# Causal masks of latent attention as a minimum on VectorE, a bf16 bias product, and three changes of order

## The chip, the cores and the metric

One Trainium2 chip, eight cores. Each core computes half of the positions (16 blocks of 128 out of 32) of one of the four sequences; there is no traffic between cores. The metric is the device time of the slowest core in microseconds.

## The reference

A decoder block on x of shape (4, 4096, 1024), float32:

```python
h = modulate(rmsnorm(x, ln_mix_g), sh1, sc1)          # shifts and scales from silu(c) @ ada_w
proj = h @ w_in                                       # q_lat 256, kv_lat 128, k_rope 32, q/k/v of the window branch, two gates of 1024
y_mla = mla_attention(...)                            # 8 heads, causal over all 4096 positions, keys 64 + 32 rotary, values 64
y_swa = swa_attention(...)                            # 16 heads, window of 128, sinks and a relative bias
merged = sigmoid(gl_a + b) * (y_mla @ w_o_mla) + sigmoid(gl_b + b) * (y_swa @ w_o_swa)
x = x + ga1 * (merged @ w_o)
h = modulate(rmsnorm(x, ln_mlp_g), sh2, sc2)
x = x + ga2 * (square(relu(h @ w_ff1)) @ w_ff2)
return rmsnorm(x, ln_final_g)
```

Latent attention masks as `where(k_idx <= q_idx, s, -inf)` ahead of its softmax.

## The kernel before

Everything lies transposed, channels on the partitions and positions on the free axis, in one SBUF arena whose addresses are planned by the phase in which each buffer lives (`Arena`). A helper class `Sched` records each operation with what it reads and writes and makes the semaphore waits, so that nearly all of an engine's instructions carry one line of the helpers: `mm` L468, `act` L473, `tt` L477, `ts` L486 and L492, `stt` L496, `cp` L500; the reciprocal is L1045, and DMAs are L276. Two stretches (the start up to the end of the x groups, and the keys and queries of the window branch) are captured and put in order by a list scheduler with modelled costs (`arrange`); elsewhere each engine runs in the order of the program text. The stages, with their times in the trace:

1. **Start and x groups, 0 to 148 us.** Adaptation weights `ada0[0..3]` (each 1 MB as bf16, from 2 MB in HBM) and blocks of x (`x_load(i)`, the same size, four buffers, own and other halves in turn) come through GpSimd's queue; small tensors, the weights `wkvxf` (1.8 MB, f32) and table copies through SP's. `ada_mm(i)` makes four columns of `modT`: i = 2, 3 give the scale, from which `wx` (scaled bf16 weights) is made, and i = 0, 1 the shift `sh1`. `bvk` is the bias that the shift adds to the latent projections: 64 f32 matmuls of one column on `wkvxf`. `x_group(i)` makes the mean square of a block with ones-matmuls, projects it by `wx`, normalizes, and builds keys, values and queries of head pair 0. An own group takes about 56 matmuls of 512 columns, the other kind about half.
2. **Latent attention, 148 to 458 us.** For each head pair j, each group c of 512 queries and each head e, the keys come in units of two tiles of 128 (own, other). `mla_front(k)` makes the scores of unit k and `act(..., Exp)` the exponentials `Pt` (bf16); `mla_back(k)` multiplies with the values, three units later in TensorE's order. Three score buffers of two PSUM banks each turn, so front k+3 waits for exponential k. A tile (j, c, e) has 4c full units and three on the diagonal: 1024 columns, 768 (two of 384), and 768 with four key tiles. Each of their eight key tiles has a mask, a further matmul `ident_bf` by `masks[mk]` (128 columns) into the scores: 0 above, −30000 below the diagonal, or a whole tile of either. When a tile ends, VectorE takes the reciprocal of the sums and scales (c even, and pair 3), or ScalarE does it by Ln and Exp. Between the units `do_step` builds the keys, values and queries of the next pair in the accumulator bank that is free, one matmul group and one or two VectorE copies each, placed by modelled times (`pe_t`, `dve_t`). GpSimd makes `ho` (`ho_step`) and the halo (`halo_step`), each one a tensor_tensor and a tensor_scalar of 1024 columns.
3. **Keys and queries of the window branch, 458 to 506 us. Window attention, 506 to 650 us.** 32 rounds `r` of four score banks, four exponentials, Ln and Exp. Rounds 0 to 15 also hold a tile of queries for the second half, rounds 16 to 27 a `gate_tile`: eight matmuls of 512 columns into bank 7 and a copy to `graw`.
4. **Merge, 650 to 850 us.** For each m of 8 output blocks and each g: the gates' matmuls (8 for each of two gates, left out where `graw` holds them, `2 * m + x < 3`), 4 and 8 matmuls of the branches, sigmoids, products.
5. **Output product, 850 to 890 us, and channel mixer, 890 to 1345 us.** `h2_apply(g)` normalizes the residual for the mixer: for each of 8 kc a VectorE product into PSUM bank 6 or 7 and a ScalarE scale and shift into `h2`. That of g = 3 lies between the first `ff1_tile`s: one kc after tile 2, 3, ... 10. An `ff1_tile` is 8 matmuls, Relu on ScalarE into `rl`, a square on VectorE; the buffer of `rl` and the bank of `h2_apply` are chosen by one shared counter `rctr`. The tiles of the first weights go by g, so tile 12 is the first that reads `h2` of g = 3.
6. **Final norm and store, to 1358 us**, through the staging buffer `ost`.

Of the kernel before, what the change touches and what calls it, by code (L numbers as in the profile page):

```python
# [17 lines left out]
NEG = -30000.0  # L18
EPOCH = 3000
# [308 lines left out]
class Arena:  # L328
# [38 lines left out]
    def solve(self):  # L367
# [14 lines left out]
        for _ in range(400):  # L382
# [15 lines left out]
def build_program(plan=None):  # L398
# [31 lines left out]
    with ExitStack() as st:  # L430
# [124 lines left out]

        def kc_src(w, c0, c1):
            return w.rearrange("(kc p) n -> p kc n", p=128)[:, :, c0:c1]
# [6 lines left out]
        S.dma("sp", hv, hv_d, "c4", writes=["hv"])  # L564
        S.dma("sp", relT[0:32, :], relT_d, "c5", writes=["relT"])
        S.dma("sp", eoh[0:32, :], eoh_d, "c6", writes=["eoh"])
        for gg in range(2):
            S.dma("sp", esink[64 * gg:64 * gg + 64, :], sinks_d[:, 8 * gg:8 * gg + 8].partition_broadcast(64), "c8",
                  writes=["esink"], group=True)
# [28 lines left out]
        o_mask = A.alloc(3 * 128 * 2, 0, 3.5, "masks")  # L598
# [66 lines left out]
        bvk = cons(F32, 4)  # L665
        blk_of = ((0, 0, 128), (1, 128, 128), (2, 256, 128), (3, 384, 64))
# [9 lines left out]
        act(esink, esink, AF.Exp, ["esink"], ["esink"])  # L676
# [300 lines left out]

        def v_lhs(t, h):
            return Vb[(h // 2) % 2][:, t, 64 * (h % 2):64 * (h % 2) + 128]
# [14 lines left out]
        def mla_front(k):  # L994
# [4 lines left out]
            for (t, off, w, qo, mk) in u:  # L999
                out = PS(sb + off // 512)[:, off % 512:off % 512 + w]  # L1000
                kd = [("Kpe0", 0, t // 4), ("Kdup0", t // 4)] if b == 0 else [("Kpe1", e, t // 4)]
                mm(out, Kb[b][e][:, 128 * t:128 * t + 128], qt[:, 512 * c + qo:512 * c + 512], True, mk is None,
                   [("K%d" % b, e, t // 4), qk + (c, 0), qk + (c, 1)] + kd,
                   [("ps", sb + off // 512)])
                if mk is not None:
# [11 lines left out]
            act(dst, src, AF.Exp, [("ps", sb), ("ps", sb + 1)], [("P", pi)], scale=SC_MLA)  # L1017

# [143 lines left out]
        o_gr = A.alloc(12 * 512 * 4, 4.6, 5, "graw")  # L1162
        graw = V(o_gr, F32, 12 * 512, [12, 512])
# [121 lines left out]
        for r in range(34):  # L1285
            if r < 32:
# [7 lines left out]
                elif r < 28:  # L1294
# [20 lines left out]
        for m in range(8):  # L1315
# [5 lines left out]
            for g in range(4):  # L1321
# [19 lines left out]
                for x, (gt, gk) in enumerate(((gA, "gA"), (gB, "gB"))):  # L1341
                    if 2 * m + x < 3:
# [35 lines left out]

        def h2_apply(g, kcs=range(8)):
            cs = slice(512 * g, 512 * g + 512)  # L1380
            for kc in kcs:
                rb = rctr[0] % 2
                rctr[0] += 1
                tt("dve", PS(6 + rb)[:, :], x1[:, kc, cs], rst[g % 2], ALU.mult, [("x1", g, kc), ("rst", g % 2)],
                   [("ps", 6 + rb)])
                act(h2[:, kc, cs], PS(6 + rb)[:, :], AF.Identity, [("ps", 6 + rb), "mod2"], [("h2", g)],
                    scale=gm2[:, kc:kc + 1], bias=sh2[:, kc:kc + 1])
# [33 lines left out]
        o_ost = A.alloc(2 * 8 * 512 * 4, 9, 9, "ost")  # L1421
# [29 lines left out]
        for hf in range(4):  # L1451
            pa, pbb = PI_FF[hf]
            for i4 in range(2):
# [167 lines left out]
```

How the kernel before makes its waits and increments, by code:

```python
                def body(eng):  # L312
                    for (waits, fn, sig) in self.prog[e]:
                        for (k, v) in waits:
                            eng.wait_ge(self.sems[k], v)
                        if fn is None:
                            continue
                        ins = fn(eng)
                        if sig is not None:
                            ins.then_inc(self.sems[sig[0]], sig[1])
```

## Time and profile before

| what | us |
| --- | --- |
| median of three runs | 1360.99 (1359.23 to 1580.57) |
| the profiled execution, its own time | 1360.09 |
| its span, first to last instruction, slowest core | 1358.5 |
| spans of the eight cores | 1353.1 to 1358.5 |
| TensorE busy | 1252.3 (92%) |
| ScalarE busy | 649.8 (48%) |
| VectorE busy | 627.5 (46%) |
| GpSimd busy | 200.4 (15%) |

TensorE's busy time counts a matmul from its first column to a modelled end and so looks fuller than it is; the distance from one matmul to the next is the better measure. All rows are those of core 5, the slowest. PEclk is the granted TensorE clock as a share of 2.4 GHz.

### The profile page before, as it was taken

How to read it: one execution, taken by the hardware profiler on the slowest of the kernel's cores; microseconds unless marked ns; L12 is line 12 of the kernel's file. 1: busy time of each engine (PE TensorE's matmuls, PEld its weight loads, DVE VectorE, ACT ScalarE, POOL GpSimd, SP SyncE). 2: the span in 40 equal slices, each digit the busy share in tenths (PEclk: the TensorE clock that was granted, in tenths of full speed). 3: DMA queues.
4: the chain of work that ended last, by engine and by line, in shares of the span. 5: the costliest groups of instructions: out<-in, count | busy, mean ns of one | idle time of the engine just before them, and what ended most of it. 6: DMA issues, size and time to landing. Idle time of an engine off the chain costs nothing.

```text
span 1358.5 us, 20199 instructions; the slowest of 8 cores (1353.1 to 1358.5 us)
## 1 busy us (share of the span) xinstructions
PE 1252.3 (92%) x6826; PEld 588.7 (43%) x6826; DVE 627.5 (46%) x849; ACT 649.8 (48%) x924; POOL 200.4 (15%) x174
## 2 busy tenths in 40 slices
PE   0599798999999999998899999979999999999997
PEld 0344344445454553332344444434444444444445
DVE  0549665655565333444322223653443443443457
ACT  0258788889889417777322223853003103202343
POOL 3000355310045001000342320010000000000000
PEclk9889899999999999999899999999999999999999
DMA  9993756130283206020462333383223205000015
GB/s 170 213 122 55 136 135 125 48 63 1 32 119 83 33 0 55 1 28 34 97 76 28 32 59 93 94 118 69 31 26 68 31 1 92 3 1 1 1 62 187
DMA packets 97507, 89.12 MB, mean 66 GB/s; under 512 B 37200, under 2 KB 83072, under 8 KB 97280
## 3 DMA queue, kind: packets, MB, share of 16 engines
q0 software_dynamic: 72640, 51.03, 28.3%
q1 hardware_dynamic: 24768, 36.81, 8.5%
q8 instruction: 58, 0.95, 0.3%
q14 instruction: 41, 0.34, 0.1%
HBM read 127.02 MB, written 8.41 MB: 100 GB/s over the span
## 4 chain that ended last, share of the span: by engine, by line
PE 85%; DVE 5%; ACT 4%; issue 4%; DMA 2%; SPq 1%; DVEq 0%; ACTq 0%; POOL 0%; POOLq 0%
PE psb L468 85%; ACT arena L473 3%; DVE arena L477 2%; DVE arena L496 1%; DMA arena<-sinks 1%; DVE arena L1045 1%; SPq L276 1%; DVE psb L477 0%; DMA scr<-arena 0%; DVE arena L500 0%; ACT L473 0%; DVE arena L486 0%; DVEq L315 0%; ACTq L315 0%; POOL arena L477 0%
## 5 line engine op out<-in xcount | busy, mean ns | idle before, releaser
L468 PE MATMUL psb<-arena 128*128 128x512 bf16 (+7 forms) x6826 | 1252.3, 347 | 98.4 <-ACT arena L473 52.8
L468 PEld LDWEIGHTS psb<-arena 128*128 128x128 bf16 (+3 forms) x6826 | 588.7, 101 | 761.8 <-issue 216.0
L473 ACT ACTIVATE arena<-psb 128x1024 bf16<-128x1024 f32 (+5 forms) x595 | 434.2, 787 | 413.9 <-PE psb L468 411.0
L477 DVE TENSOR_TENSOR arena<-psb,arena 128x512 f32<-128x512 f32 (+2 forms) x222 | 145.1, 660 | 276.3 <-ACT arena L473 181.4
L477 DVE TENSOR_TENSOR arena<-arena 128x512 bf16<-128x512 f32 (+3 forms) x150 | 111.1, 742 | 159.8 <-ACT arena L473 159.3
L496 DVE SCALAR_TENSOR_TENSOR arena<-psb,arena 128x512 f32<-128x512 f32 (+1 forms) x168 | 121.8, 725 | 136.0 <-PE psb L468 135.8
L473 ACT ACTIVATE arena<-arena 128x512 f32<-128x512 f32 (+4 forms) x211 | 139.3, 675 | 89.0 <-DVE arena L496 63.8
L473 ACT ACTIVATE arena<-psb,arena 128x512 f32<-128x512 f32 (+2 forms) x113 | 79.9, 709 | 156.9 <-PE psb L468 143.2
L500 DVE CAST arena<-psb 64x512 bf16<-64x512 f32 (+1 forms) x134 | 92.1, 688 | 86.2 <-PE psb L468 84.9
L477 POOL TENSOR_TENSOR arena<-arena 128x512 bf16<-128x512 f32 (+1 forms) x56 | 96.9, 1730 | 229.3 <-DVE arena L477 113.0
L1045 DVE RECIPROCAL arena<-psb 64x512 f32<-64x512 f32 x20 | 67.1, 3355 | 26.5 <-PE psb L468 25.9
L276 POOL DMA_DIRECT2D arena<-w_ff x16 | 13.0, 822 | 309.0 <-PE psb L468 248.3
L496 DVE SCALAR_TENSOR_TENSOR arena<-arena 128x512 f32<-128x512 f32 (+6 forms) x75 | 53.8, 728 | 8.1 <-ACT arena L473 3.8
L276 POOL DMA_DIRECT2D arena<-win x19 | 17.2, 909 | 150.7 <-PE psb L468 150.7
L276 POOL DMA_DIRECT2D arena<-ada_w x12 | 11.0, 918 | 165.8 <-PE psb L468 165.0
L492 POOL TENSOR_SCALAR arena<-arena 128x1024 bf16<-128x1024 f32 x24 | 29.1, 1214 | 5.8 <-POOL arena L477 3.9
L473 ACT ACT_TABLE_LOAD x5 | 6.4, 1283 | 42.3 <-DMA arena<-sinks 29.8
L477 DVE TENSOR_TENSOR psb<-arena 128x512 f32<-128x512 f32 x32 | 21.9, 692 | 0.3 <-ACT arena L473 0.3
L500 DVE COPY arena<-psb 128x512 f32<-128x512 f32 (+3 forms) x22 | 12.9, 586 | 19.7 <-PE psb L468 19.7
L486 DVE TENSOR_SCALAR arena<-arena 128x448 bf16<-128x448 f32 (+4 forms) x19 | 9.6, 533 | 3.9 <-ACT arena L473 3.1
L276 POOL DMA_DIRECT2D arena<-xo x4 | 3.6, 892 | 52.1 <-PE psb L468 52.1
L500 DVE CAST arena<-arena 128x1024 f32<-128x1024 int32 (+1 forms) x3 | 3.5, 1157 | 11.6 <-DMA arena<-pos 11.4
(14 smaller groups left out, 32.9 us busy)
## 6 DMA issues: line engine op xcount, KB each, us to landing
arena<-w_ff POOLq DMA_DIRECT2D x16, 1024.0 KB, 10.9
arena<-ada_w POOLq DMA_DIRECT2D x12, 1024.0 KB, 15.1
arena<-xo SPq DMA_DIRECT2D x16, 512.0 KB, 4.8
arena<-xo SPq DMA_DIRECT2D x4, 2048.0 KB, 8.1
out<-arena SPq DMA_DIRECT2D x12, 512.0 KB, 3.0
arena<-xo POOLq DMA_DIRECT2D x4, 1024.0 KB, 29.5
arena<-xs POOLq DMA_DIRECT2D x4, 1024.0 KB, 31.9
arena<-xs SPq DMA_DIRECT2D x8, 512.0 KB, 4.4
```

Of the source, the lines that this page charges most:

```text
L276: return eng.dma_start(out=out, in_=in_, **kw)
L468: S.op("pe", lambda e: e.matmul(out, lhsT=lhsT, rhs=rhs, start=start, stop=stop), reads=R, writes=Wr, sig=sig, cost=cost_of("pe", out, lhsT))
L473: S.op("act", lambda e: e.activation(out=out, in_=in_, func=func, **kw), reads=R, writes=Wr, cost=cost_of("act", out))
L477: S.op(eng, lambda e: e.tensor_tensor(out=out, in0=in0, in1=in1, op=op), reads=R, writes=Wr, cost=cost_of(eng, out, in0, in1))
L486: is not None else e.tensor_scalar(out=out, in0=in0, scalar1=s1, scalar2=None, op0=op0),
L492: S.op(eng, lambda e: e.tensor_scalar(out=out, in0=in0, scalar1=s1, scalar2=s2, op0=op0, op1=op1), reads=R, writes=Wr, cost=cost_of(eng, o ...
L496: S.op("dve", lambda e: e.scalar_tensor_tensor(out=out, in0=in0, scalar=scalar, in1=in1, op0=op0, op1=op1), reads=R, writes=Wr, cost=cost_ ...
L500: S.op(eng, lambda e: e.tensor_copy(out=out, in_=in_), reads=R, writes=Wr, cost=cost_of(eng, out, in_))
L1045: S.op("dve", lambda e_, ab=ab, hy=hy, hs=hs: e_.reciprocal(out=R[hy, :], in_=PS(ab)[hs, :]), reads=[("ps", ab)], writes=[("rr", e)])
```

## The change

- In latent attention, groups c = 1, 2, 3 lose their mask matmuls. In their place `cap` takes the elementwise minimum of the exponentials and a table `caps`, which holds 0 where a key is hidden and the largest bf16-sized number elsewhere. It is a VectorE tensor_tensor of 128 x 256 bf16, in place on `Pt`, right behind the exponential: one on each of the first two diagonal units and two on the third. Group c = 0 keeps its masks. `caps` is made once by four small tensor_scalars.
- In the start, the small SP loads (with `sinks`) go ahead of `wkvxf`; `x_load(1)` goes ahead of `ada0` 0 and 1; `bvk` is made from a bf16 copy of the weights (two ScalarE copies) and a shift split into two bf16 parts, 32 bf16 matmuls of two columns, summed by two VectorE reductions; the exponential of the sinks waits for `bvk`.
- Window rounds 28 to 31 take gate tiles too, so the merge leaves four gates out of m = 0 and 1.
- `h2_apply(3)`: the VectorE product runs two kc ahead of the ScalarE part, with its own bank choice, no longer through `rctr`.
- `ost` takes the place of `h2`; the arena's search may take more trials.

```diff
-        S.dma("sp", wkvxf, kc_src(win_d, 0, QC + KVC), "wkvx", writes=["wkvxf"])
         S.dma("sp", hv, hv_d, "c4", writes=["hv"])
...
+        S.dma("sp", wkvxf, kc_src(win_d, 0, QC + KVC), "wkvx", writes=["wkvxf"])
...
-        x_load(0)
+        for i in range(2):
+            x_load(i)
         for i in (0, 1):
             ada0_load(i)
-        for i in range(1, NXB):
+        for i in range(2, NXB):
             x_load(i)
...
+        for q in range(2):
+            act(wkvb[:, 4 * q:4 * q + 4, :], wkvxf[:, 4 * q:4 * q + 4, :], AF.Copy, ["wkvxf"], [("wkvb", q)])
+        cp("dve", sh1s[:, :, 0], sh1, [("mod", 0), ("mod", 1)], [("sh1s", 0)])
+        tt("dve", sh1s[:, :, 1], sh1, sh1s[:, :, 0], ALU.subtract, [("mod", 0), ("mod", 1), ("sh1s", 0)], [("sh1s", 1)])
         for (col, c0, M) in blk_of:
             for kc in range(8):
-                mm(PS(6)[0:M, col:col + 1], wkvxf[:, kc, c0:c0 + M], sh1[:, kc:kc + 1], kc == 0, kc == 7,
-                   ["wkvxf", ("mod", 0), ("mod", 1)], [("ps", 6)])
-            cp("dve", bvk[0:M, col:col + 1], PS(6)[0:M, col:col + 1], [("ps", 6)], ["bvk"])
+                mm(PS(6)[0:M, 2 * col:2 * col + 2], wkvb[:, kc, c0:c0 + M], sh1s[:, kc, :], kc == 0, kc == 7,
+                   [("wkvb", kc // 4), ("sh1s", 0), ("sh1s", 1)], [("ps", 6)], sig=(kc == 7 and col == 3))
...
-        act(esink, esink, AF.Exp, ["esink"], ["esink"])
+        act(esink, esink, AF.Exp, ["esink", "bvk"], ["esink"])
...
+        for sl, mk in ((0, 0), (1, 1), (2, 0), (3, 2)):
+            ts("dve", caps[:, sl // 2, sl % 2, :], masks[:, mk, :], 0.0, BIG, ALU.is_ge, ALU.mult, ["masks"], ["caps"])
+
+        def cap(pi, off, step, sel):
+            v = Pt[pi][:, off:off + 2 * step].rearrange("p (a b) -> p a b", a=2)[:, :, 0:128]
+            tt("dve", v, v, caps[:, sel, :, :], ALU.min, [("P", pi), "caps"], [("P", pi)])
...
-                if mk is not None:
+                if mk is not None and c == 0:
                     mm(PS(sb + off // 512)[:, off % 512:off % 512 + 128], ident_bf, masks[:, mk, :], False, True,
                        ["ident", "masks"], [("ps", sb + off // 512)])
...
             act(dst, src, AF.Exp, [("ps", sb), ("ps", sb + 1)], [("P", pi)], scale=SC_MLA)
+            if c > 0 and len(u) == 2 and u[0][4] is not None:
+                cap(pi, 0, 512, u[1][4] - 1)
+            elif c > 0 and len(u) == 4:
+                cap(pi, 0, 256, 0)
+                cap(pi, 512, 128, 1)
...
-                elif r < 28:
+                elif r < 32:
                     q = r - 16
                     gate_tile(q // 8, q % 4, q // 4 % 2)
...
-                        if 2 * m + x >= 3:
+                        if 2 * m + x >= 4:
...
                     if hf == 0 and i4 == 0 and 3 <= n_ < 11:
-                        h2_apply(3, (n_ - 3,))
+                        if n_ == 3:
+                            h2_norm(3, 0)
+                            h2_norm(3, 1)
+                        h2_shift(3, n_ - 3)
+                        if n_ - 1 < 8:
+                            h2_norm(3, n_ - 1)
```

## Rows read from the trace of the kernel before

**Rows 1.** The page: busy us of each engine, its share of the span, instructions
```profile
PE 1252.3 (92%) x6826; PEld 588.7 (43%) x6826; DVE 627.5 (46%) x849; ACT 649.8 (48%) x924; POOL 200.4 (15%) x174
```
**Rows 2.** Busy time by stage: stretch, its length, then each engine's us (instructions)
```profile
core 5: us, PE busy (x) PEld busy (x) DVE busy (x) ACT busy (x) POOL busy (x), PEclk, DMA share, GB/s
0.00:71.80 71.80, 24.05 (x210) 16.91 (x210) 19.28 (x31) 11.49 (x11) 12.51 (x21) 0.92 1.08 190
148.00:458.00 310.00, 289.23 (x1970) 150.41 (x1968) 177.11 (x186) 273.23 (x307) 99.41 (x65) 0.99 0.44 83
890.00:930.00 40.00, 32.94 (x143) 14.12 (x142) 16.47 (x25) 17.28 (x29) 3.66 (x5) 0.91 0.91 137
```
**Rows 3.** Waits from 148 to 458 us: engine line waited for, us, times, longest
```profile
ACT arena L473 <- PE psb L468: 33.4, 68, 1.7
```
**Rows 4.** Groups by form from 148 to 458 us: count, busy us, mean ns
```profile
L473 ACT ACTIVATE arena<-psb 128x1024 bf16<-128x1024 f32 x224 | 214.4, 1037 | 27.3 <-PE psb L468 25.8
L477 POOL TENSOR_TENSOR arena<-arena 128x1024 f32<-128x1024 f32 x24 | 56.4, 2351 | 41.2 <-DMA arena<-xo 22.7 <-DMA arena<-xs 18.3
L492 POOL TENSOR_SCALAR arena<-arena 128x1024 bf16<-128x1024 f32 x24 | 29.1, 1214 | 5.8 <-POOL arena L477 3.9 <-PE psb L468 1.9
```
**Rows 5.** TensorE in order of time from 1200 us: start, us, matmuls
```profile
1199.71 85.63 PE L468 MATMUL psb<-arena 128*128 128x512 bf16 x396
```
**Rows 6.** VectorE groups by form over the span: count, busy us, mean ns
```profile
L477 DVE TENSOR_TENSOR arena<-arena 128x2048 bf16<-128x2048 bf16 x8 | 9.7, 1218 | 0.1
L477 DVE TENSOR_TENSOR arena<-psb,arena 128x4 f32<-128x4 f32 x12 | 1.9, 160 | 42.0 <-PE psb L468 42.0
```
**Rows 7.** A tile of c = 1, pair 2, in order of time, 319.6 to 323.9 us
```profile
318.33 3.35 DVE L1045 RECIPROCAL arena<-psb 64x512 f32<-64x512 f32 x1
319.73 4.66 ACT L473 ACTIVATE arena<-psb 128x1024 bf16<-128x1024 f32 x5 [1.22 <-PE psb L468]
321.78 0.69 DVE L477 TENSOR_TENSOR arena<-psb,arena 64x512 bf16<-64x512 f32 x1
```
**Rows 8.** The two-SBUF-input VectorE product in 311 to 314 and in 233 to 237 us
```profile
L477 DVE TENSOR_TENSOR arena<-arena 64x512 bf16<-64x512 f32 x1 | 0.7, 684 | 3.3 <-ACT arena L473 3.3
L477 DVE TENSOR_TENSOR arena<-arena 64x512 bf16<-64x512 f32 x1 | 2.5, 2509 | 3.2 <-ACT arena L473 3.2
```
**Rows 9.** The start in order of time, 0 to 165 us
```profile
29.77 1.28 ACT L473 ACT_TABLE_LOAD   x1 [29.77 <-DMA arena<-sinks]
61.80 3.54 PE L468 MATMUL psb<-arena 128*128 128x1 f32 x16 [2.31 <-DVE arena L477]
82.09 1.62 PEld L468 LDWEIGHTS psb<-arena 128*128 128x128 bf16 x9 [0.41 <-issue]
89.28 1.90 ACT L473 ACTIVATE arena<-arena 128x2048 bf16<-128x2048 bf16 x1
```
**Rows 10.** The load of x block 2 (issued at 6.90 us): KB, us to landing
```profile
arena<-xo POOLq DMA_DIRECT2D x1, 1024.0 KB, 62.8
```
**Rows 11.** ScalarE in order of time: window rounds 24, 28 and 31 begin
```profile
612.27 2.06 ACT L473 ACTIVATE arena<-psb 128x512 bf16<-128x512 f32 x4 [1.21 <-PE psb L468]
...
629.74 2.07 ACT L473 ACTIVATE arena<-psb 128x512 bf16<-128x512 f32 x4 [1.21 <-PE psb L468]
...
639.43 2.05 ACT L473 ACTIVATE arena<-psb 128x512 bf16<-128x512 f32 x4
```
**Rows 12.** The mixer's first tiles: waits from 890 to 930 us, then order of time
```profile
PE psb L468 <- ACT arena L473: 7.0, 2, 6.1
909.80 0.69 DVE L477 TENSOR_TENSOR psb<-arena 128x512 f32<-128x512 f32 x1
912.62 0.69 DVE L477 TENSOR_TENSOR psb<-arena 128x512 f32<-128x512 f32 x1
917.20 9.00 PE L468 MATMUL psb<-arena 128*128 128x512 bf16 x32 [6.09 <-ACT arena L473]
```
**Rows 13.** TensorE group of one-column bf16 matmuls over the span: count, busy us, mean ns
```profile
L468 PE MATMUL psb<-arena 128*128 128x1 bf16 x384 | 11.4, 163 | 37.8 <-ACT arena L473 36.1 <-DVE arena L477 1.3
```

More of the change, by code:

```diff
@@ L18 @@
 NEG = -30000.0
+BIG = float(2.0 ** 128 - 2.0 ** 120)
 EPOCH = 3000
@@ L381, in solve @@
         order = list(best[2])
-        for _ in range(400):
+        for _ in range(3000):
             if best[0] <= self.limit:
@@ L554, in build_program @@
         S.dma("sp", gains, gains_d, "c2", writes=["gains"])
+        S.dma("sp", hv, hv_d, "c4", writes=["hv"])
+        S.dma("sp", relT[0:32, :], relT_d, "c5", writes=["relT"])
+        S.dma("sp", eoh[0:32, :], eoh_d, "c6", writes=["eoh"])
+        for gg in range(2):
+            S.dma("sp", esink[64 * gg:64 * gg + 64, :], sinks_d[:, 8 * gg:8 * gg + 8].partition_broadcast(64), "c8",
+                  writes=["esink"], group=True)
         def kc_src(w, c0, c1):
@@ L563, in build_program @@
         S.dma("sp", wkvxf, kc_src(win_d, 0, QC + KVC), "wkvx", writes=["wkvxf"])
[L564 to L569, printed above, removed]
         o_ada0 = A.alloc(4 * 8192, 0, 0, "ada0")
@@ L590, in x_load @@
                   ("xst", i % NXB), writes=[("xst", i % NXB)])
-        x_load(0)
+        for i in range(2):
+            x_load(i)
         for i in (0, 1):
             ada0_load(i)
-        for i in range(1, NXB):
+        for i in range(2, NXB):
             x_load(i)
         S.dma("pool", ident_bf, ident_d, "c9", writes=["ident"])
-        o_mask = A.alloc(3 * 128 * 2, 0, 3.5, "masks")
+        o_mask = A.alloc(7 * 128 * 2, 0, 3.5, "masks caps")
+        caps = V(o_mask + 3 * 128 * 2, BF16, 4 * 128, [2, 2, 128])
         masks = V(o_mask, BF16, 3 * 128, [3, 128])
@@ L668, in build_program @@
             for kc in range(8):
-                mm(PS(6)[0:M, col:col + 1], wkvxf[:, kc, c0:c0 + M], sh1[:, kc:kc + 1], kc == 0, kc == 7,
-                   ["wkvxf", ("mod", 0), ("mod", 1)], [("ps", 6)])
-            cp("dve", bvk[0:M, col:col + 1], PS(6)[0:M, col:col + 1], [("ps", 6)], ["bvk"])
+                mm(PS(6)[0:M, 2 * col:2 * col + 2], wkvb[:, kc, c0:c0 + M], sh1s[:, kc, :], kc == 0, kc == 7,
+                   [("wkvb", kc // 4), ("sh1s", 0), ("sh1s", 1)], [("ps", 6)], sig=(kc == 7 and col == 3))
+        for (c0, c1, M) in ((0, 3, 128), (3, 4, 64)):
+            S.op("dve", lambda e, c0=c0, c1=c1, M=M: e.reduce_sum(
+                out=bvk[0:M, c0:c1], in_=PS(6)[0:M, 2 * c0:2 * c1].rearrange("p (a b) -> p a b", b=2),
+                axis=mybir.AxisListType.X), reads=[("ps", 6)], writes=["bvk"], cost=0.2)
         mm(PS(6)[0:16, 0:128], relT[0:32, :], eoh[0:32, :], True, True, ["relT", "eoh", "bvk"], [("ps", 6)])
@@ L1161, in build_program @@
         qsT = [V(o, BF16, 4 * T, [4, T]) for o in o_qs]
[L1162 to L1163 removed]
+        o_gr = A.alloc(16 * 512 * 4, 4.6, 5, "graw")
+        graw = V(o_gr, F32, 16 * 512, [16, 512])
         ksT = V(o_ks, BF16, T)
@@ L1377, in tail_ones, with h2_norm, h2_shift @@
             act(rst[q % 2][:, 0:w], rst[q % 2][:, 0:w], AF.Exp, [("rst", q % 2)], [("rst", q % 2)], scale=-0.5)
+        def h2_norm(g, kc):
+            cs = slice(512 * g, 512 * g + 512)
+            tt("dve", PS(6 + kc % 2)[:, :], x1[:, kc, cs], rst[g % 2], ALU.mult, [("x1", g, kc), ("rst", g % 2)],
+               [("ps", 6 + kc % 2)])
+        def h2_shift(g, kc):
+            act(h2[:, kc, 512 * g:512 * g + 512], PS(6 + kc % 2)[:, :], AF.Identity, [("ps", 6 + kc % 2), "mod2"],
+                [("h2", g)], scale=gm2[:, kc:kc + 1], bias=sh2[:, kc:kc + 1])
         def h2_apply(g, kcs=range(8)):
-            cs = slice(512 * g, 512 * g + 512)
             for kc in kcs:
[L1382 to L1387, printed above, removed]
+                h2_norm(g, kc)
+                h2_shift(g, kc)
         xre_load(1)
@@ L1420, in build_program @@
         it2 = 0
-        o_ost = A.alloc(2 * 8 * 512 * 4, 9, 9, "ost")
+        o_ost = o_h2
+        if S.live:
+            S.region(o_ost, 2 * 8 * 512 * 4, ["ost"])
         def final_apply(q, kcs=range(8)):
```

7 lines of the change are left out of this document (5 added, 2 removed).

## The prediction

> **What bounds the kernel now.** I read the page first, then busy time by stage, then the waits and the order of time inside the stages that the change touches. The page has TensorE busy for 92% of the span and no other engine above 48% [rows 1]. So work saved on TensorE counts wherever TensorE is the engine that the others wait for, and the question for each edit is whether it is so in its stage.
>
> By stage [rows 2]: up to 71.8 us TensorE is busy for only 24 us while the DMA share is 1.08, so the start waits for data. Latent attention, 148 to 458 us, has TensorE busy for 289 of 310 us and ScalarE for 273 us, so two engines are near their limit there. From 890 to 930 us TensorE has 7 us of idle time and a mean granted clock of 0.91 of 2.4 GHz. The waits of latent attention say which of the two engines leads: ScalarE waited 33.4 us for TensorE's scores, in 68 waits [rows 3]. TensorE leads, by some 10% of the stage, and gains less once ScalarE's exponentials (1024 columns in 1.04 us, 224 of them, 214 us busy [rows 4]) become the pace.
>
> **Masks (groups 1 to 3).** 8 mask matmuls in each tile, 3 groups, 8 heads: 192 matmuls of 128 columns. 396 matmuls of 512 columns take 85.63 us [rows 5], 0.216 us each, so 128 columns take 0.054 us, and 192 take 10.4 us. All of it is on TensorE's queue. ScalarE has on average 33.4 / 24 = 1.4 us of waiting per tile of these groups to give up, more than the 0.43 us saved, so I count the 10.4 us in full before the costs below.
>
> The minimum: the trace has no such instruction. The nearest are a bf16 product of 2048 columns, 1.218 us, and a sum of 4 columns, 0.160 us [rows 6]. The line through both gives 0.29 us for 256 columns. The bounds are 0.16 us and, for full f32 speed, the 0.68 us of a 512-column product with both inputs in SBUF [rows 8]. I take 0.29, as the type and kind are those of the first row. 96 of them are 28 us on VectorE, which is busy 177 of 310 us [rows 2], so there is room on average. What counts is the delay of `mla_back(k)`, which now waits for exponential and minimum. Between front k and back k TensorE issues three fronts and three backs, 12 matmuls of 0.216 us or 2.6 us, and the exponential uses 1.04 us of it. That leaves 1.5 us for 0.29 us (0.6 us for the two of the last unit). Even where ScalarE leads, front k+3 (0.43 us) still stands between. With an idle VectorE the minimum costs nothing.
>
> VectorE is not always idle. Two cases can cost:
> - *Behind a reciprocal.* In the tile (c = 1, e = 0) the reciprocal of the group-0 tile lies ahead: it starts at 318.33 and takes 3.35 us, its scaling ends at 321.78 + 0.69 = 322.47 [rows 7]. The first diagonal exponential is the first of the five from 319.73, so it ends about 320.75, and its back matmul comes about 1.4 us later, at 322.1. With the minimum it can start at 322.8: 0.7 us late. Four pairs give 2.8 us; the tile (c = 1, e = 1) of pair 3, which also follows a reciprocal, 0.6 us more. Longer tiles have eight or more full units first, time enough for 4.1 us. Sum 3.4 us.
> - *Behind GpSimd.* The same VectorE product takes 0.684 us in one place and 2.509 us where GpSimd is inside a tensor_tensor [rows 8]. GpSimd's two instructions are 2.35 and 1.21 us long, 24 of each in this stage [rows 4], 86 of 310 us, and lie mostly in 160 to 246 us and in pair 3. There, 52 minima meet a busy GpSimd with a chance of about a half; a hold of up to 2.35 us exceeds the slack of 1.2 us that is left in a minority, by some tenths. I take 3 us, between 0 (all hidden) and 31 us (third rival).
>
> Behind a waiting minimum stand the copies of `do_step`. The next tile's first back, which needs their bank, comes four iterations later, over 3 us, so they cost nothing while that holds. `caps` is four small instructions in an idle stretch: nothing. Latent attention: −10.4 + 3.4 + 3.0 = **−4.0 us**.
>
> The Trainium skill (GPSIMD Engine Reference, section on specifications) says that GpSimd shares its SBUF interfaces with VectorE and contends with VectorE instructions that have two SBUF inputs; the minimum is one. The trace agrees with its 2.509 us.
>
> **The start.** ScalarE's first instruction waits 29.77 us for `sinks`, because these lie behind `wkvxf`, and with it wait `scT`, all `ada_mm` and the table chain of VectorE [rows 9]. Then x group 0 runs; the bias takes 4 x 3.54 us of f32 matmuls from 61.80 to about 75.8; only then x group 1; and the ones-matmuls of group 2 start at 82.09 [rows 9]. In the new order x groups 0 and 1 are through, and the bias is 32 bf16 matmuls of 11.4 / 384 = 0.03 us [rows 13], 1 us in all. The two copies of weights are at most 1.9 us each [rows 9] on an idle ScalarE. What sets the time next is the landing of x block 2: 6.90 + 62.8 = 69.7 us [rows 10]. The same bytes lie ahead of it as before and the DMA share is full up to there, so it doesn't move. With the square of half a block, 1.9 us [rows 9], its ones-matmuls start at 71.8, 10.3 us earlier. TensorE will have idled for some microseconds before, and then steps at half speed at first, as at 917.20, where 32 matmuls took 9.00 us [rows 12] and 32 x 0.216 = 6.9 would do: 2.1 us lost. **−8.2 us.** Bounds: 0 (the planner leaves the order as it was or data come later) and −14 us (the f32 bias alone, everything else in its shadow).
>
> **Gates in rounds 28 to 31.** Rounds with a gate take (629.74 − 612.27) / 4 = 4.37 us, without one (639.43 − 629.74) / 3 = 3.23 us, there ScalarE leads [rows 11]. Four rounds grow by 1.14 us, 4.5 us. The merge loses four groups of 8 x 0.216 us, 6.9 us. **−2.4 us**; at worst 0, at best −6.9.
>
> **The mixer's first tiles.** One kc of `h2_apply` costs 912.62 − 909.80 = 2.82 us, a closed loop of VectorE, ScalarE, Relu and square, against 8 x 0.216 = 1.73 us of an `ff1_tile`. TensorE so waits 7.0 us for ScalarE, and the slow restart at 917.20 loses 2.1 us [rows 12]. With the product two kc ahead, each engine has two instructions per tile, about 1.3 to 1.4 us, below 1.73. So TensorE no longer waits: **−9.1 us**. At worst half is left, −4.5. The stages behind are full of TensorE, nothing later eats it.
>
> `ost` on `h2`, whose last readers are long done, costs nothing; nor does the arena's search.
>
> **Sum.** 4.0 + 8.2 + 2.4 + 9.1 = 23.7 us from 1360.1 us of the profiled execution (span 1358.5): **1336 us**. The median shown, 1361, is 0.9 us above that execution, no more. The change is 1.8%. A measurement of this kernel tells about 2% from no change, that is below 1334 us or above 1388 us.
>
> **Rivals.**
> 1. *VectorE hides all minima.* For it: 1.5 us of slack. Against it: the reciprocal ahead [rows 7]. Then latent attention gives 10.4, in sum 30.1: 1330 us.
> 2. *The start gives nothing*, since the data or the halved clock set it or the list scheduler places the groups otherwise. For it: the DMA share of 1.08 [rows 2]. Against it: group 1 stood 14 us behind the bias. 1336.4 + 8.2: 1345 us.
> 3. *Slower: GpSimd holds the minima.* GpSimd is inside an instruction for 86 / 310 = 28% of the stage; 96 minima, with a mean rest of about 1.1 us, are 30 us of holds if none is hidden. Latent attention then costs −10.4 + 3.4 + 30 = +23, in sum 1360.1 − 19.7 + 23 = 1363 us. It decides where the slack behind the exponential is below the hold; TensorE's lead over ScalarE makes the slack, and the change takes that lead away. Against it: in three fifths of the stage GpSimd is idle.
> 4. *`h2_apply` keeps half of its stall*, as the squares of the tiles come in between on VectorE: 1341 us.
>
> The rule of the Trainium skill on the shared interfaces (GPSIMD Engine Reference, specifications) is the mechanism of the third rival, and would make it 1363 us if it bit each time.
>
> **Chances.** Forecast 0.55 (its own range 1329 to 1344), rival 1 0.18, rival 2 0.13, rival 3 0.05, rival 4 0.09. Leaving out rival 3 and the tails, the range is **1326 to 1349 us**. Faster by over 2%: rival 1 at 0.15 of its 0.18, and 0.19 of the forecast: 0.34. Slower by over 2%: 0.01. Within: 0.65.
>
> **What would show it.** Right: no mask matmuls beyond c = 0 (64 in all, of 256); latent attention about 306 us long; ScalarE's wait for TensorE well under 33 us; minima of 0.29 us, a few of 2 us; x group 2 at about 72 us; rounds 28 to 31 of 4.4 us; no TensorE wait near 905 us. Wrong: minima behind which TensorE waits in most tiles; latent attention as long as before; x group 2 later than 76 us.

## The result, and the profile after

The changed kernel takes 1371.32 us in the median of 5 runs (1368.48 to 1515.14), the kernel before 1359.97 us (1357.88 to 1580.57) beside it. The ratio is 1.008, with a 95% interval of 1.0061 to 1.0099: 0.8% **slower**, little but clearly apart from no change, and not the 1336 us of the forecast. Some executions of any kernel here are disturbed on some cores and take up to 16% longer; every ratio is taken from undisturbed ones, and where they spoil a median, the lowest time stands in its place.

The profiled execution took 1369.8 us, with a span of 1368.1 us on core 4. The cores lie between 1361.0 and 1368.1 us, so it isn't one late core. The page, busy us of each engine, its share and instructions, to be held against [rows 1]:

```profile
PE 1238.9 (91%) x6602; PEld 567.0 (41%) x6602; DVE 664.9 (49%) x953; ACT 651.2 (48%) x925; POOL 201.2 (15%) x174
```

TensorE has 224 instructions and 13.4 us of work less, and the kernel got longer: the difference is waiting. Which stage it is in shows when each core's span is cut at ScalarE's first and last exponential of latent attention (medians over the eight cores, read from ScalarE's order of time):

| us | up to it | latent attention | behind it |
|---|---|---|---|
| before | 148.9 | 305.3 | 901.4 |
| after | 141.2 | 333.1 | 890.0 |
| forecast of the change | −8.2 | −4.0 | −11.5 |
| measured change | −7.7 | **+27.8** | −11.4 |

Two of three stages come out nearly as forecast. Latent attention, where the mask matmuls were taken away, is 32 us off. Its busy time by stage in the changed kernel (columns as in [rows 2], second window chosen to hold the whole stage of core 4):

```profile
148.00:458.00 310.00, 261.80 (x1615) 126.72 (x1614) 205.83 (x268) 249.75 (x281) 93.90 (x60) 0.98 0.36 73
143.00:478.00 335.00, 286.41 (x1766) 139.34 (x1766) 213.58 (x284) 272.43 (x307) 99.37 (x64) 0.98 0.37 73
```

TensorE was idle 310.00 − 289.23 = 20.8 us in the stage before [rows 2] and is idle 335.00 − 286.41 = 48.6 us now: 27.8 us more. What it waits for, from the waits of the stage (us, times, longest), first in the kernel before, 148 to 458 us:

```profile
PE psb L468 <- DVE arena L477: 11.0, 8, 1.9
PE psb L468 <- ACT arena L473: 8.1, 10, 1.1
```

and in the changed kernel, 145 to 478 us:

```profile
ACT arena L474 <- PE psb L469: 58.5, 65, 4.5
DVE arena L478 <- ACT arena L474: 49.1, 35, 5.1
PE psb L469 <- DVE arena L501: 22.0, 20, 3.3
PE psb L469 <- DVE arena L478: 16.7, 14, 1.9
PE psb L469 <- ACT arena L474: 7.3, 9, 1.1
```

Line 501 is a copy of the projections that `do_step` builds between the attention tiles; line 478 is the helper of the products and of the minima. TensorE didn't wait for such a copy before and now does so 20 times, 22.0 us in all. That is TensorE's largest new row, and it doesn't name the minimum. (ScalarE's 58.5 us, against 33.4 in [rows 3], reads as the echo: its scores come late because TensorE does, as in the rows below.)

One such place in the order of time of the changed kernel (start, us, engine and line, count, then the wait before it):

```profile
338.94 0.29 DVE L478 TENSOR_TENSOR arena<-arena 128x256 bf16<-128x256 bf16 x1 [2.90 <-ACT arena L474]
339.64 0.29 DVE L478 TENSOR_TENSOR arena<-arena 128x256 bf16<-128x256 bf16 x1 [0.41 <-ACT arena L474]
339.86 0.68 DVE L501 CAST arena<-psb 128x512 bf16<-128x512 f32 x1
340.69 1.67 PE L469 MATMUL psb<-arena 128*128 128x512 bf16 x7 [1.69 <-DVE arena L501]
341.86 1.02 ACT L474 ACTIVATE arena<-psb 128x1024 bf16<-128x1024 f32 x1 [1.61 <-PE psb L469]
```

VectorE stands 2.90 us at a minimum whose exponential isn't there yet, then 0.41 us at the next. Only behind them does it reach the copy of a build, at 339.86. TensorE, which needs the bank that this copy empties, has stood 1.69 us when it goes on, and ScalarE 1.61 us for its scores. GpSimd has no part in it. Here it has one:

```profile
430.00 1.41 DVE L501 CAST arena<-psb 64x512 bf16<-64x512 f32 x2 [0.63 <-PE psb L469]
432.07 2.91 DVE L478 TENSOR_TENSOR arena<-arena 128x256 bf16<-128x256 bf16 x2 [0.67 <-ACT arena L474]
432.46 2.37 POOL L478 TENSOR_TENSOR arena<-arena 128x1024 f32<-128x1024 f32 x1
435.01 0.69 DVE L501 CAST arena<-psb 128x512 bf16<-128x512 f32 x1
435.85 4.35 PE L469 MATMUL psb<-arena 128*128 128x512 bf16 x16 [3.16 <-DVE arena L501]
437.44 1.02 ACT L474 ACTIVATE arena<-psb 128x1024 bf16<-128x1024 f32 x1 [4.22 <-PE psb L469]
```

Two minima that need 0.29 us each take 2.91 us; they end at 434.98, just behind GpSimd's tensor_tensor (432.46 + 2.37 = 434.83). The copy starts at 435.01, and TensorE has waited 3.16 us for it.

The three copies of this place read PSUM and take their usual 0.7 us, the first two beside another tensor_tensor of GpSimd (428.78 to 431.13 us). A third cost shows in the clock that TensorE was granted behind its wait (columns as in [rows 2]):

```profile
435.30:438.60 3.30, 2.75 (x7) 1.09 (x8) 2.62 (x5) 1.02 (x1) 2.65 (x2) 0.50 0.39 116
```

This is the lower of the two levels, 1.2 GHz. It came at 435.25 us, while TensorE stood idle.

### The profile page after: what moved, and what is told of

It is laid out like the page before. It is cut to its first block, busy times and chain, and to the rows that moved or that the text cites. A ratio compares the mean times of both kernels' runs of the same rounds, so it can differ in the third digit from the quotient of the medians.

```text
span 1368.1 us, 19972 instructions; the slowest of 8 cores (1361.0 to 1368.1 us)
## 1 busy us (share of the span) xinstructions
PE 1238.9 (91%) x6602; PEld 567.0 (41%) x6602; DVE 664.9 (49%) x953; ACT 651.2 (48%) x925; POOL 201.2 (15%) x174
## 4 chain that ended last, share of the span: by engine, by line
PE 80%; DVE 6%; ACT 5%; issue 5%; DMA 3%; another core or an unknown queue 1%; POOL 0%; ACTq 0%; DVEq 0%; POOLq 0%; SPq 0%
PE psb L469 80%; ACT arena L474 5%; DMA arena<-xo 2%; DVE arena L478 2%; DVE arena L501 2%; DVE arena L1071 1%; DVE arena L497 1%; DMA scr<-arena 0%; POOL arena L277 0%; ACTq L316 0%; DVEq L316 0%; ACT L474 0%; POOL arena L478 0%; POOLq L316 0%
## 5 line engine op out<-in xcount | busy, mean ns | idle before, releaser
L469 PE MATMUL psb<-arena 128*128 128x512 bf16 (+6 forms) x6602 | 1238.9, 351 | 121.4 <-DMA arena<-ada_w 28.7
L469 PEld LDWEIGHTS psb<-arena 128*128 128x128 bf16 (+1 forms) x6602 | 567.0, 99 | 793.1 <-issue 250.3
L478 DVE TENSOR_TENSOR arena<-arena 128x512 bf16<-128x512 f32 (+4 forms) x247 | 149.5, 611 | 195.2 <-ACT arena L474 180.3
L474 ACT ACTIVATE arena<-arena 128x512 f32<-128x512 f32 (+6 forms) x217 | 145.0, 684 | 127.7 <-DVE arena L497 53.3
L474 ACT ACTIVATE arena<-psb,arena 128x512 f32<-128x512 f32 (+2 forms) x109 | 76.9, 709 | 133.3 <-PE psb L469 130.6
L497 DVE SCALAR_TENSOR_TENSOR arena<-arena 128x512 f32<-128x512 f32 (+6 forms) x75 | 53.9, 727 | 12.8 <-ACT arena L474 8.4
L501 DVE COPY arena<-psb 128x512 f32<-128x512 f32 (+1 forms) x22 | 15.0, 681 | 6.3 <-PE psb L469 6.3
L504 POOL MEMSET arena<- 128x2048 bf16 (+4 forms) x6 | 4.3, 779 | 24.7 <-PE psb L469 20.2
L501 DVE CAST arena<-arena 128x1024 f32<-128x1024 int32 (+2 forms) x4 | 2.2, 562 | 11.4 <-DMA arena<-pos 11.2
```

Of the source, the lines that this page charges most:

```text
L469: S.op("pe", lambda e: e.matmul(out, lhsT=lhsT, rhs=rhs, start=start, stop=stop), reads=R, writes=Wr, sig=sig, cost=cost_of("pe", out, lhsT))
L474: S.op("act", lambda e: e.activation(out=out, in_=in_, func=func, **kw), reads=R, writes=Wr, cost=cost_of("act", out))
L478: S.op(eng, lambda e: e.tensor_tensor(out=out, in0=in0, in1=in1, op=op), reads=R, writes=Wr, cost=cost_of(eng, out, in0, in1))
L497: S.op("dve", lambda e: e.scalar_tensor_tensor(out=out, in0=in0, scalar=scalar, in1=in1, op0=op0, op1=op1), reads=R, writes=Wr, cost=cost_ ...
L501: S.op(eng, lambda e: e.tensor_copy(out=out, in_=in_), reads=R, writes=Wr, cost=cost_of(eng, out, in_))
L504: S.op(eng, lambda e: e.memset(ap, val), writes=Wr)
```

## The experiments

Times are medians. The interval of a ratio is about ±0.002 (from ±0.001 to ±0.005), or 3 us, and a difference between two kernels is good to 3 or 4 us. The kernel before gave 1359.9 to 1360.5 us beside all of them.

**One part at a time.** The theory: the minimum costs, the other edits give what was forecast. First the changed kernel with its mask matmuls back in all groups and no minima:

```diff
-                if mk is not None and c == 0:
+                if mk is not None:
...
-            if c > 0 and len(u) == 2 and u[0][4] is not None:
-                cap(pi, 0, 512, u[1][4] - 1)
-            elif c > 0 and len(u) == 4:
-                cap(pi, 0, 256, 0)
-                cap(pi, 512, 128, 1)
```

> The changed kernel with the mask matmuls of groups 1 to 3 put back and the minima left out; all other parts of the change stay. The two traces put latent attention 26 us longer after the change, the start 5 to 8 us shorter and everything behind latent attention 12 us shorter. If these are separate, this kernel takes 1360 - 7 - 12 = 1341 us. If the longer latent attention came with the new start (other data in flight, a shifted clock) and not from the minima, it stays near 1366 us.

Its lowest time is 1338.07 us (of 1338.07 to 1561.92), and it has no interval. The same kernel once more:

> The kernel of the first experiment again (all of the change but the minima), for its interval on the chip of this group: 1339 us, ratio to the kernel before 0.985.

Measured: 1340.21 us (1339.87 to 1341.37), ratio 0.9848 (0.9834 to 0.9863). This beats both kernels, and puts the price of minima against masks at 1371.3 − 1340.2 = **31.1 us**. TensorE's waits in it, 145 to 478 us (which holds some 30 us behind its latent attention), are those of before, with no wait for a copy among them:

```profile
PE psb L469 <- DVE arena L478: 9.4, 6, 1.8
PE psb L469 <- ACT arena L474: 8.1, 10, 1.1
```

The opposite, the kernel before with only the minimum in place of the masks of groups 1 to 3:

> The kernel before with the minimum in place of the mask matmuls of groups 1 to 3 and nothing else of the change. If the minima cost what the traces say, 1360 + 26 = 1386 us. If the loss needs the other parts, 1356 us as forecast for this edit alone.

Measured: ratio 1.0275 (1.0235 to 1.0315), by which it takes about 1397 us; the lowest time is 1393.5 us. Latent attention has a median of 335.5 us over the cores, and the same new row:

```profile
PE psb L469 <- DVE arena L501: 23.0, 21, 3.1
PE psb L469 <- DVE arena L478: 22.8, 16, 3.1
```

And neither masks nor minima in groups 1 to 3. This leaves out the causal mask there, so its time is that of a kernel in which masking is free:

```diff
-            if c > 0 and len(u) == 2 and u[0][4] is not None:
-                cap(pi, 0, 512, u[1][4] - 1)
-            elif c > 0 and len(u) == 4:
-                cap(pi, 0, 256, 0)
-                cap(pi, 512, 128, 1)
```

> The changed kernel with neither mask matmuls nor minima in groups 1 to 3 (the causal mask of these groups is left out: keys ahead of a query are not hidden there). It prices the 192 matmuls alone. If TensorE leads latent attention as forecast, 10.4 us less than with the masks back: 1331 us. If ScalarE's exponentials take over as the pace, only a part: 1336 us or more.

Measured: 1336.42 us, ratio 0.9822 (0.9806 to 0.9839). So 192 mask matmuls, 10.4 us of TensorE, are worth 1340.2 − 1336.4 = **3.8 us** of time (3.5 us by the two ratios, good to 3 us; 4.8 us by the stage, 306.7 against 301.9 us). Masking on another engine could have gained about that and no more.

**What in the minimum costs: a ladder.** Rival theories: VectorE's time, GpSimd's holds, VectorE's wait for the exponential with the copies behind it, TensorE's wait for the minimum. They are put on one by one. First, with the masks back, 96 minima of the same shape that read only the table and write to a scratch tile: they wait for no exponential, and no result of theirs is read.

```diff
-            tt("dve", v, v, caps[:, sel, :, :], ALU.min, [("P", pi), "caps"], [("P", pi)])
+            tt("dve", scrap, caps[:, sel, :, :], caps[:, sel, :, :], ALU.min, ["caps"], ["scrap"])
```

> The kernel with the masks back and, at the places of the changed kernel, 96 VectorE minima of the same size that read the table alone and write a scratch tile: they wait for no exponential and nothing waits for them. It prices VectorE's time and what GpSimd does to it. Theory queue (VectorE waits at the minimum for its exponential, and what is queued behind it comes late): these minima cost little, 1340 to 1345 us against some 1339 with the masks back. If VectorE's mere load or GpSimd's holds make the loss: 1355 us or more.

Measured: 1352.4 us, ratio 0.9944 (0.9923 to 0.9966): **+12.2 us** for instructions whose result nobody reads, between the two times expected. Their row by form (count, busy us, mean ns):

```profile
L478 DVE TENSOR_TENSOR arena<-arena 128x256 bf16<-128x256 bf16 x96 | 46.5, 484 | 6.4 <-DVE arena L478 0.5
```

Fourteen of the 96 take 22.8 us together (11 to 15 of them and 15.9 to 22.8 us on the eight cores). Then the same, but reading the real exponentials, still writing to the scratch tile, so that VectorE waits for ScalarE while TensorE doesn't wait for the minimum:

```diff
+            tt("dve", scrap, v, caps[:, sel, :, :], ALU.min, [("P", pi), "caps"], ["scrap"])
```

> As the run before, but the 96 minima read the exponentials and write the scratch tile: VectorE waits for each exponential, and no matmul waits for a minimum. Theory queue: most of the loss comes back, 1358 to 1370 us. If the loss is TensorE waiting for the minimum itself (it comes too late for its matmul), this kernel stays at 1340 to 1347 us.

Measured: 1368.86 us, ratio 1.0059 (1.0041 to 1.0076): **+16.5 us** more. TensorE's wait for the copies is there nearly in full, although no matmul reads a minimum:

```profile
PE psb L469 <- DVE arena L501: 19.4, 21, 3.2
PE psb L469 <- ACT arena L474: 14.3, 16, 2.0
ACT arena L474 <- DVE arena L478: 6.9, 5, 2.0
```

The third row is a side effect of the experiment: the scratch minimum still reads the exponentials' buffer, and the exponential that fills this buffer next waits until it has. So this step isn't VectorE's waiting alone. The run without GpSimd's products, below, has no such wait.

The last step, real minima and no masks, is 1371.3 − 1368.9 = +2.4 us. With 3.8 us of matmuls saved, 6.2 us are left for TensorE waiting for the minimum itself; that is a remainder of small differences and not measured by itself.

**Is the 12.2 us GpSimd's?** The changed kernel without GpSimd's 24 tensor_tensors in this stage (left out: the multiplication by the reciprocal root for `ho` and the halo):

> The changed kernel without GpSimd's 24 tensor_tensors of 2.35 us in latent attention (the multiplication of the two normalized inputs by their reciprocal root is left out; GpSimd's tensor_scalars stay). In the changed trace 15 of 96 minima are longer than 0.4 us, 19.5 us together where 0.29 us each would be 4.4. If all of these holds reach TensorE: 1370 - 12 = 1358 us. If the queue hides them: 1368 us.

Measured: 1357.8 us, ratio 0.9979 (0.9969 to 0.9989), −13.5 us; the minima now

```profile
L478 DVE TENSOR_TENSOR arena<-arena 128x256 bf16<-128x256 bf16 x96 | 29.4, 318 | 36.2 <-ACT arena L474 33.4
```

and TensorE's wait for the copies

```profile
PE psb L469 <- DVE arena L501: 18.5, 20, 1.7
```

318 ns in the mean for 446 in the changed kernel, while the number of waits for a copy is 20 as before and only the longest fell, from 3.3 to 1.7 us. Three controls with the same work left out: masks back and no minima; masks back with the idle minima; and with the scratch minima.

> The kernel with the masks back, and GpSimd's 24 tensor_tensors left out as in the third run of the last group: the control for it. If those instructions cost nothing without the minima, 1340 us, and the 13.5 us that they cost the changed kernel are holds of minima. If they cost as much here (the two scalings of e = 0 that they also hold), below 1335 us.

> The kernel with 96 idle minima (no wait, no reader) without GpSimd's tensor_tensors. With them the idle minima cost 12.2 us over the masks back. If that is GpSimd's holds, 1342 us. If it is VectorE's time (28 us of instructions between the others), 1352 us as before.

> The kernel with masks back and 96 minima that read the exponentials and write a scratch tile, without GpSimd's tensor_tensors: VectorE's wait for the exponentials alone, no holds, no matmul behind a minimum. Idle minima gave 1338.7 us here. Theory queue: the wait costs the same 16 us as with GpSimd's instructions, 1355 us. If wait and hold only hurt together: 1343 us.

| us | with GpSimd's products | without |
|---|---|---|
| masks, no minima | 1340.2 | 1337.5 |
| idle minima added | 1352.4 (+12.2) | 1338.7 (+1.2) |
| they wait for exponentials | 1368.9 (+16.5) | 1355.0 (+16.3) |
| real ones, no masks | 1371.3 (+2.4) | 1357.8 (+2.8) |

The ratios of the last column are 0.9838 (0.9822 to 0.9853), 0.9849 (0.9833 to 0.9864), 0.9964 (0.9943 to 0.9985) and 0.9979. By the ratios, times 1360 us, the three steps are 13.1, 15.6 and 2.9 us with the products and 1.5, 15.6 and 2.0 us without, each good to 3 or 4 us: the steps of 1 to 3 us aren't told apart from nothing, the others are. So of the 12.2 us, some 11 us come with GpSimd's products, and VectorE's waiting costs some 16 us with and without them. The two costs add. That the 16 us come by way of the copies shows in the run without products, where neither a minimum nor a held instruction makes ScalarE wait:

```profile
PE psb L469 <- DVE arena L501: 15.7, 21, 1.5
```

The 11 us aren't only the holds themselves. With the idle minima the granted clock from 150 to 440 us is 0.98 or 0.99 on all eight cores; with the products left out it is 1.00 on all eight (the slowest core of each):

```profile
150.00:440.00 290.00, 261.66 (x1752) 134.73 (x1751) 203.69 (x266) 244.85 (x274) 89.92 (x58) 0.98 0.43 77
150.00:440.00 290.00, 270.01 (x1847) 139.44 (x1845) 195.70 (x271) 256.97 (x289) 38.70 (x37) 1.00 0.48 79
```

By an estimate from these rows, 0.01 to 0.02 of 290 us are 3 to 6 us of TensorE's time; with the masks back and no minima the clock is 0.99 or 1.00. So by this estimate up to about 5 of the 11 us are the lower clock that came with the holds.

**The minimum later on VectorE's queue.** If VectorE stands at the minimum because it is issued too early, it should be enough to put it behind the work of the next two units:

```diff
+            if 0 <= k - 2 < len(units):
+                mla_cap(k - 2)
             if k >= LA:
```

> The changed kernel with each minimum put into VectorE's queue two units later in the program (one unit ahead of the matmuls that read it), so that its exponential is nearly done when VectorE reaches it. Theory queue: VectorE stands at the minimum until the exponential ends, the copies of the next pair's builds wait behind it, and TensorE waits for their bank. Then most of the 27 us of added TensorE waits go, and it takes 1340 to 1350 us. Rivals reciprocal and GpSimd: the minimum itself comes too late, behind a reciprocal or held by a GpSimd instruction. Then putting it later doesn't help or makes it worse: 1368 us or more.

Measured: ratio 1.0079 (1.0056 to 1.0103), 1371.4 us in the lowest run. No gain, where the queue theory alone would have 1340 to 1350 us. The waits show a trade:

```profile
PE psb L469 <- DVE arena L478: 36.1, 34, 3.0
PE psb L469 <- DVE arena L501: 1.8, 7, 0.5
```

The wait for the copies went from 22.0 to 1.8 us, as the theory has it, and that for line 478, the minima among it, from 16.7 to 36.1 us: now the minimum stands behind the copies and reciprocals, and the value matmuls behind it. Without GpSimd's products the same place gave

> The changed kernel with each minimum two units later in VectorE's queue and GpSimd's tensor_tensors left out. The later place alone changed nothing (1371 us), leaving out the tensor_tensors alone gave 1358 us. Theory: the later minimum frees the build copies, but has so little time left before its matmul that each hold by GpSimd reaches TensorE. Then both together leave little of the loss: 1342 us. If the later minimum is late without GpSimd too, behind the copies: 1352 to 1358 us.

1355.76 us, ratio 0.9961 (0.9945 to 0.9977), 2 us below the 1357.8 of the early place, which is within the noise, and far from the 1342 that the first theory expected. So it isn't the holds that make it late. Between the two, one unit later:

> The changed kernel with each minimum one unit later in VectorE's queue. A compromise between the place right behind the exponential (1371 us, build copies wait) and two units later (1371 us, TensorE waits for minima): 1363 us if both fade, 1371 us if they only trade.

1360.95 us, ratio 1.0014 (0.9996 to 1.0033): −10.4 us (−9.0 us by the ratios). Both waits are there, each smaller (the sum of the two is 31.9 us, against 38.7 and 37.9):

```profile
PE psb L469 <- DVE arena L478: 27.8, 27, 3.3
PE psb L469 <- DVE arena L501: 4.1, 10, 1.0
```

**Which tiles.** Masks back in group 1, where the reciprocal lies close ahead, minima only in groups 2 and 3, 64 of the 96:

```diff
-                if mk is not None and c == 0:
+                if mk is not None and c <= 1:
...
-            if c > 0 and len(u) == 2 and u[0][4] is not None:
+            if c > 1 and len(u) == 2 and u[0][4] is not None:
...
```

> The changed kernel with mask matmuls in group 1 too; the minima stay in groups 2 and 3 (64 of 96), whose tiles have eight or twelve full units between a reciprocal and the first minimum. If every minimum costs alike, a third of the 31 us goes: 1361 us. If those behind a reciprocal are the dear ones, 1350 us. If groups 2 and 3, where most builds of the next pair lie, carry the loss: 1366 us.

Measured: 1358.53 us, ratio 0.9992 (0.9981 to 1.0003), −12.8 us. A third of the minima carries 12.8 / 31.1 = 41% of the cost, which the noise of 3 to 4 us doesn't tell apart from a third. Most of the cost lies in the two groups whose tiles the forecast had cleared of the reciprocal by "time enough": there it isn't the reciprocal.

**The other edits.** The norm two ahead alone, on the kernel before:

> The kernel before with the one edit that the mixer's VectorE product runs two blocks ahead of ScalarE's part. As forecast: 9.1 us less, 1351 us. If another wait takes its place, half of it: 1355 us.

Measured: 1351.06 us, ratio 0.9935 (0.9913 to 0.9956), −9.0 us; the time behind latent attention falls from 901.4 to 891.4 us. Then masks back and the last gate tiles back in the merge, and as its control the kernel with the masks back alone, on the same chip:

```diff
-                elif r < 32:
+                elif r < 28:
...
-                        if 2 * m + x >= 4:
+                        if 2 * m + x >= 3:
```

> The kernel after with the mask matmuls back and the last four gate tiles back in the merge; only the new start and the two-ahead norm are left. If gates are worth 2.4 us and the start 8.2 as forecast, about 1342.6 us (1340.2 + 2.4; ratio 0.987). If the late rounds' gates give nothing, 1340.2. If the start gave only the 4.4 us that the slowest core's trace shows, the gates would be worth the rest of the 10.8, 6.4 us, and this gives 1346.6.

> The same kernel as e8 on the chip of e16, so that the two stand side by side: 1340 us, ratio 0.985.

Measured: 1337.19 us (1335.23 to 1350.51), ratio 0.9852 (0.9798 to 0.9906), and 1339.74 us, ratio 0.9861 (0.9839 to 0.9882): not told apart in time. The stages tell why. Behind latent attention the kernel without the late gates needs 891.9 us, the control 888.1: the gates give 3.8 us there. But up to latent attention it needs 135.4 us, the control 140.1. TensorE at the start (start, us, count, wait before it), control first, core 4 of each:

```profile
50.06 1.89 PE L469 MATMUL psb<-arena 128*128 128x512 bf16 x8 [2.26 <-ACT arena L474]
57.28 0.99 PE L469 MATMUL psb<-arena 128*128 128x1 bf16 x32 [5.33 <-DMA arena<-ada_w]
```

```profile
48.99 7.14 PE L469 MATMUL psb<-arena 128*128 128x512 bf16 x24 [2.56 <-ACT arena L474]
58.79 0.94 PE L469 MATMUL psb<-arena 128*128 128x1 bf16 x32 [2.66 <-DMA arena<-ada_w]
```

The planned order differs: 16 matmuls more run ahead of the wait for `ada_w`. The size of `graw`, 24 or 32 KB, is all that the edit changes in what is planned that early; by which rule the plan turned on it stays open. It means that the start edit can give up to 148.9 − 135.4 = 13.5 us, and gives 6.9 and 8.8 us in the two traces of the kernel with the late gates and the masks back.

## Why the prediction was wrong

- **Masks, −10.4 us "in full": wrong in size.** Worth 3.8 us. The ground given, that ScalarE has 1.4 us of waiting to give up in each tile, was an average over the stage. Without any mask ScalarE gave up less than 3 us of it, from 32.2 us (70 waits, masks back, 143 to 450 us) to this (142 to 445 us), and TensorE began to wait for copies:

```profile
ACT arena L474 <- PE psb L469: 29.5, 56, 2.0
PE psb L469 <- DVE arena L501: 1.5, 7, 0.4
```

  So it isn't shown that ScalarE's pace is what took the rest; where most of the missing 6.6 us went stays open.
- **The minimum's duration, 0.29 us: right.** On the slowest core the 81 short ones take 0.288 us in the mean.
- **"Behind a waiting minimum stand the copies of `do_step` … so they cost nothing while that holds": the step that failed.** It cost some 16 us, the largest term. The forecast looked at the next reader of the bank in the attention tiles, "four iterations later, over 3 us", and not at the next build. By the code that places them, 54 of the 72 builds come one or two units behind another on the same accumulator bank, so the second build's matmuls wait for the first one's copy, and on TensorE's queue the attention tiles' matmuls wait behind them. Two units are 8 matmuls of 0.216 us, 1.7 us, while VectorE stood at minima 29 times for 32.4 us in the changed kernel, with 2.90 us as the longest ahead of a copy. (The two longest of all, 5.13 us, lie in the last tiles, where there are no builds.) The forecast named the instructions queued behind the new wait, and then excused them with one reader out of two.
- **GpSimd's holds, +3 us between 0 and 31: too small.** They cost some 11 us, with the clock that falls behind them. The step that put them "in a minority, by some tenths" took only the value matmul as the one who waits. 15 of the 96 minima are over 0.4 us on the slowest core and take 19.5 us together (8 to 15 and 11.5 to 22.8 us on the eight cores), a minority indeed, but whole holds, and the idle minima show that what they delay is what stands behind them on VectorE. The forecast had no term for the clock here. The third rival named this mechanism, its 1363 us being for a full count of 30 us, and had a chance of 0.05; as "slower" the result is nearest to it, though for a mechanism of which it was only the smaller half.
- **Behind a reciprocal, +3.4 us: the mechanism right, the size rather small.** In each of the four pairs TensorE waits for the minimum of the tile (c = 1, e = 0) right behind the scaling: 1.21, 1.29, 1.10 and 1.10 us, 4.7 us for the 2.8 us forecast. The trace with scratch minima has no wait at these places. In pair 2, in order of time:

```profile
331.98 0.69 DVE L478 TENSOR_TENSOR arena<-psb,arena 64x512 bf16<-64x512 f32 x1
332.70 1.09 DVE L478 TENSOR_TENSOR arena<-arena 128x256 bf16<-128x256 bf16 x4
333.14 5.85 PE L469 MATMUL psb<-arena 128*128 128x512 bf16 x34 [1.10 <-DVE arena L478]
```

  The tile (c = 1, e = 1) of pair 3 has 1.86 us, but the scratch minima have 1.82 us there for the exponential. The remainder of the ladder, 6.2 us, fits; the reciprocal's part wasn't measured alone in time.
- **The start, −8.2 us: right in size, in part by luck.** −7.7 us. Block 2's square starts at 70.76 us, for 69.7 forecast (to which 1.9 us add up to 71.6, not the 71.8 written):

```profile
70.76 1.91 ACT L474 ACTIVATE arena<-arena 128x2048 bf16<-128x2048 bf16 x1 [18.16 <-DMA arena<-xo]
67.48 7.64 PE L469 MATMUL psb<-arena 128*128 128x512 bf16 x48 [1.56 <-DVE arena L478]
```

  But of x group 1 much is in the stretch from 67.48 us, not through before the bias as was assumed; e16 has it earlier, and its first stage is 4.7 us shorter still (140.1 against 135.4 us). The forecast didn't see either order.
- **Gates, −2.4 us: right, as far as the stages tell.** Round 28 begins at 651.78 and round 31 at 664.74 us, 3 rounds in 12.96 us or 4.32 each (forecast 4.37; [rows 11] had 3.23), and the time behind latent attention gains 3.3 us by e11 and 3.8 us by e16. In the time of the whole kernel it isn't told apart from nothing.

```profile
651.78 2.06 ACT L474 ACTIVATE arena<-psb 128x512 bf16<-128x512 f32 x4 [1.20 <-PE psb L469]
...
664.74 2.06 ACT L474 ACTIVATE arena<-psb 128x512 bf16<-128x512 f32 x4 [0.93 <-PE psb L469]
```

- **The mixer's first tiles, −9.1 us: right.** −9.0 us alone, mechanism and size. Where [rows 2, 12] have 32.94 of 40 us, a clock of 0.91 and a wait of 6.09 us, the changed kernel has TensorE busy throughout at the full granted clock:

```profile
890.00:930.00 40.00, 40.00 (x187) 18.12 (x186) 25.89 (x41) 29.52 (x45) 4.89 (x6) 1.00 0.70 102
```

The sum with the measured terms: 1360.0 − 19.8 (start, gates, mixer, from e8) − 3.8 + 6.2 + 16.5 + 12.2 = 1371.3 us. It closes by construction, as 6.2 us is the remainder. The range was too narrow for two reasons: it had no term at all for the copies, because their cost was argued to be nothing rather than bounded, and it left out the third rival, the one bound on the holds that went beyond 3 us.

Open: the kernel before with only the minimum costs 2.75%, some 37 us, where the same exchange costs 31.1 us in the changed kernel. The 6 us between them are about as large as their uncertainty (1.0235 to 1.0315 is ±5 us). Its latent attention is 335.5 us against 333.1 us, so 2.4 of the 6 us are there; the rest isn't explained. Planning the builds' copies apart from the minima (another bank, or another place in the unit) wasn't tried.

## What to carry to other kernels

Before an instruction that waits is put on an engine, list everything queued behind it on that engine and every reader of their outputs, background work and its bank reuse included; bound that cost, and don't argue it to zero with one reader. Work taken off the leading engine is worth less than its length where others are nearly as busy; one kernel that leaves the work out tells how much (here 3.8 us of 10.4) before a replacement is built. In such an experiment an instruction that writes to a scratch tile is still a reader of its inputs, and can hold up who writes them next. Where an engine in a closed loop gets a new step, its place in the queue trades one wait for another: look at both before moving it.

## What the runs showed of the hardware

In these traces a VectorE minimum with two inputs in SBUF that meets a GpSimd tensor_tensor ends only with it: 0.288 us alone, 2.91 us for a pair that meets one of 2.37 us. With GpSimd inside its two instructions for some 27% of the stage (86 of 320 us), 96 of them cost some 11 us of kernel time without anybody reading their result. The Trainium skill (GPSIMD Engine Reference, section on specifications) has this contention as a rule; the runs agree, and give its price: 484 ns in the mean, and 339 ns where GpSimd's products are left out:

```profile
L478 DVE TENSOR_TENSOR arena<-arena 128x256 bf16<-128x256 bf16 x96 | 32.5, 339 | 6.3 <-DVE arena L478 0.5
```

With the holds came a lower clock. Core 4 of the changed kernel falls to the lower of the two levels (1.2 GHz) at 172.4, 250.9 and 435.3 us, each time while TensorE stands in a wait for VectorE (3.27, 1.33 and 3.16 us) behind a held minimum (2.47, 2.43 and 2.42 us). From 155 us to the end of the stage all eight cores of the changed kernel have such a stretch, two of eight in the kernel before, and none of eight in the changed kernel without GpSimd's products, where TensorE waits for copies just as often (20 times) but for at most 1.7 us.
